# Mixture-of-experts kernel: tokens of two pairs of experts gathered at once, through a one-hot matrix of 256 columns

## What is computed

```python
def hier_moe(h, w_group, b_group, w_expert, b_expert, w1, w3, w2):
    # g_sel: best of 4 groups; e_id: best 2 of the 8 experts in that group; e_w: their weights
    y = grouped_expert_ffn(xf, e_id, w1, w3, w2)
    return einsum('nkd,nk->nd', y, e_w)

def ffn(xb, e):                       # xb: the tokens that chose expert e
    return (silu(xb @ w1[e]) * (xb @ w3[e])) @ w2[e]
```

## Time and profile before

| | us |
|---|---|
| median of 3 runs | 2134.16 (2133.64 to 2135.18) |
| span of the profiled execution | 2134.4 |
| PE busy | 2069.4 (97%) |
| DVE busy | 1592.3 (75%) |
| ACT busy | 1286.2 (60%) |
| POOL busy | 104.7 (5%) |
| mixer | up to about 1100 |
| pairs 1 to 14 | about 1181 to 2032 |
| last pair and the end | about 2032 to 2134 |

### The profile page before, as it was taken

One profiled execution on the slowest core, in us unless ns is written; L12 is line 12 of the kernel. 1 busy time (PEld: TensorE's weight loads), 2 busy tenths in 40 slices (PEclk: granted clock), 3 DMA queues, 4 the chain that ended last, 5 costly groups with the idle time before them and its releaser, 6 DMA issues.

```text
span 2134.4 us, 30028 instructions
## 1 busy us (share of the span) xinstructions
PE 2069.4 (97%) x11452; PEld 1749.8 (82%) x11452; DVE 1592.3 (75%) x1450; ACT 1286.2 (60%) x1064; POOL 104.7 (5%) x76
## 2 busy tenths in 40 slices
PE   8999999999999999999999999999999999999986
PEld 8998888899999998887887777777777787777764
DVE  7646664453646375455669999999999999999988
ACT  5445653333333323334347888888888888888883
POOL 1000000000000000001000000000000000000010
PEclk9999999999999999999999999999999999999998
DMA  6554335655454544557777999999999999999996
GB/s 215 159 139 158 118 120 186 208 180 172 146 176 148 166 157 143 192 197 239 233 297 287 399 421 421 421 420 419 418 420 418 421 418 417 417 417 418 417 397 251
DMA packets 168608, 606.48 MB, mean 284 GB/s; under 512 B 20252, under 2 KB 32684, under 8 KB 117452
## 3 DMA queue, kind: packets, MB, share of 16 engines
q1 hardware_dynamic: 164976, 598.01, 73.9%
q0 software_dynamic: 3552, 7.37, 1.1%
HBM read 595.05 MB, written 22.04 MB: 289 GB/s over the span
## 4 chain that ended last, share of the span: by engine, by line
PE 64%; DVE 16%; issue 9%; DMA 7%; ACT 3%; DVEq 0%; POOLq 0%; POOL 0%; SPq 0%; ACTq 0%
PE ps L1991 19%; PE ps L1972 15%; DVE wl L786 11%; DMA raw<-in_w_dram 7%; PE ps L1119 5%; PE ps L1120 5%; PE ps L2349 4%; PE ps L1116 3%; ACT wh L636 2%; PE ps L2104 2%; PE ps L1141 1%; DVE yall L951 1%; PE ps L2064 1%; PE ps L1089 1%; PE ps L2077 1%
## 5 line engine op out<-in xcount | busy, mean ns | idle before, releaser
L786 DVE TENSOR_TENSOR wl<-raw,wh 128x2048 fp32r<-128x2048 f32 x347 | 780.9, 2288 | 39.7 <-ACT wh L636 38.4
L636 ACT ACTIVATE wh<-raw 128x2048 fp32r<-128x2048 f32 x347 | 661.6, 1915 | 132.8 <-DMA raw<-in_w_dram 72.6
L1548 DVE TENSOR_TENSOR wl<-raw,wh 128x2048 fp32r<-128x2048 f32 (+1 forms) x168 | 379.8, 2263 | 283.3 <-ACT wh L1350 283.3
L1350 ACT ACTIVATE wh<-raw 128x2048 fp32r<-128x2048 f32 (+1 forms) x168 | 317.9, 1895 | 444.6 <-DMA raw<-in_w_in_dram 264.7
L1119 PE MATMUL ps<-wh,xg 128*128 128x512 f32 x896 | 373.1, 416 | 25.0 <-DVE wl L786 24.5
L1120 PE MATMUL ps<-wl,xg 128*128 128x512 f32 x880 | 345.2, 392 | 0.0
L1972 PE MATMUL ps<-hth,wh 128*128 128x272 f32 (+1 forms) x896 | 259.8, 290 | 3.1 <-DVE wl L1548 1.8
L1972 PE MATMUL ps<-htl,wh 128*128 128x272 f32 (+1 forms) x896 | 255.7, 285 | 0.0
L1972 PE MATMUL ps<-hth,wl 128*128 128x272 f32 (+1 forms) x896 | 255.6, 285 | 0.0
L1119 PEld LDWEIGHTS ps<-wh,xg 128*128 128x128 f32 x896 | 169.1, 189 | 77.2 <-DVE wl L786 28.3
L1119 PE MATMUL ps<-wh,hx 128*128 128x512 f32 x508 | 202.4, 398 | 3.5 <-DVE wl L786 1.9
(11 more groups left out here) (379 smaller groups left out, 3116.7 us busy)
## 6 DMA issues: line engine op xcount, KB each, us to landing
raw<-in_w_dram SPq DMA_DIRECT2D x380, 1024.0 KB, 10.4
raw<-in_w_in_dram SPq DMA_DIRECT2D x103, 1024.0 KB, 5.1
raw<-in_w_pa_dram SPq DMA_DIRECT2D x16, 1024.0 KB, 5.0
raw<-in_w_pb_dram SPq DMA_DIRECT2D x16, 1024.0 KB, 5.0
raw<-in_w_out_dram SPq DMA_DIRECT2D x16, 1024.0 KB, 5.1
raw<-in_w_ukv_dram SPq DMA_DIRECT2D x8, 1024.0 KB, 5.3
raw_e<-in_w_dram SPq DMA_DIRECT2D x4, 1024.0 KB, 8.1
yscr<-zeros SPq DMA_DIRECT2D x4, 1024.0 KB, 10.7
```

Source lines behind the costliest of these rows:

```text
L636: nc.scalar.activation(wh2[:, x % HELD, :], raw_of(turn, x), ACT.Copy).then_inc(s_wh2, 1)
L786: nc.vector.tensor_tensor(wl_of(turn, x), raw_of(turn, x), wh2[:, x % HELD, :].bitcast(F32), ALU.subtract).then_inc(s_wl2, 1)
L1350: nc.scalar.activation(wh[:, n % RING1, 0:c], raw1[:, n % RING1, 0:c], ACT.Copy).then_inc(s_wh, 1)
L1548: nc.vector.tensor_tensor(wl[:, n % RING1, 0:c], raw1[:, n % RING1, 0:c], wh[:, n % RING1, 0:c].bitcast(F32), ALU.subtract).then_inc(s_wl, 1)
```

## The change

The tokens of two pairs are gathered together, and only in pairs with an odd number n (`quad_next`): in pair 1 for pairs 2 and 3, in pair 3 for 4 and 5, up to pair 13 for 14 and 15. DVE builds one matrix of 256 columns (`gather_matrix_quad`, two operations of the old size at step 1 of an odd pair). PE does 16 portions (`gather_quad`), one for each chunk of the model width, after the steps 3 to 10 and 15 to 22 of the odd pair (`G_QUAD`); each has four matmuls of 256 columns. ACT copies each portion (`gathered_quad`) in one operation of 512 columns to two places of `xg`, which now has room for three pairs in rotation (n % 3). The pair with an even number has no gather. Pair 1 is still gathered during pair 0 in the old way.

For the rotation by three and the parity of two, the loop is written out over six pairs on PE, ACT and DVE (`cycles`, two turns), with pairs 0, 1, 14 and 15 written out before and after it. Counted in instructions of PE, weight loads included, the body of the loop grows from 1256 (two pairs) to 3389 (six pairs). Buffers move in SBUF, and `ln2g` lies where ring buffer 4 was, so that SP waits for unit 20 of the last pair before it loads it. Some waits on PE change: `mix` waits for `s_hp` and for the last portion of a gather in its banks, and the steps 0 to 3 of an even pair wait for four more chunks each.

```diff
-        xg = place("xg", [P, 2, KD, 2, 2 * SLOTS], 131072, F32R)
+        xg = place("xg", [P, 3, KD, 2, 2 * SLOTS], 131072, F32R)
-        hx = place("hx", [P, KF, 2 * SLOTS], 163840, F32R)
-        hx2 = place("hx2", [P, KF, 2 * SLOTS], 131072, F32R)
-        yall = place("yall", [P, D_MODEL], 165888)
+        hx = place("hx", [P, KF, 2 * SLOTS], 180224, F32R)
+        hx2 = place("hx2", [P, KF, 2 * SLOTS], 147456, F32R)
+        yall = place("yall", [P, D_MODEL], 196608)
...
-        selt = place("selt", [P, SEQ], 133120)
-        identr = place("identr", [P, P], 134144, F32R)
-        evens = [place("even_hi", [P, D_MODEL], 174080, F32R), place("even_lo", [P, D_MODEL], 135168, F32R)]
-        ln2g = place("ln2g", [P, D_MODEL], 196608)
+        selt = place("selt", [P, SEQ], 149504)
+        identr = place("identr", [P, P], 150528, F32R)
+        evens = [place("even_hi", [P, D_MODEL], 172032, F32R), place("even_lo", [P, D_MODEL], 151552, F32R)]
+        ln2g = place("ln2g", [P, D_MODEL], 4 * 8192)
...
-        ab = place("ab", [P, 2, FF], M0)
-        sg = place("sg", [P, 4 * SLOTS], M0 + 4096)
-        hv = place("hv", [P, KF, SLOTS], M0 + 5120)
-        zeros = place("zeros", [P, 4 * SLOTS], M0 + 5120)
-        pg = place("pg", [P, TT, 2 * SLOTS], M0 + 11712, F32R)
+        ab = place("ab", [P, 2, FF], M0 - 1024)
+        sg = place("sg", [P, 4 * SLOTS], M0 + 3072)
+        hv = place("hv", [P, KF, SLOTS], M0 + 4096)
+        zeros = place("zeros", [P, 4 * SLOTS], M0 + 4096)
+        pg = place("pg", [P, TT, 4 * SLOTS], M0 + 5120, F32R)
...
-        G_AT = (4, 6, 8, 10, 16, 18, 20, 22)
+        G_QUAD = {**{3 + c: c for c in range(8)}, **{7 + c: c for c in range(8, KD)}}
+        CYCLE = 6
+        MATRICES = 2 + (PAIRS - 2) // 2
...
+        def quad_slots(n):
+
+            return sorted((n % 3, (n + 1) % 3))
+
+        def quad_next(n, last):
+
+            return n % 2 == 1 and not last
+
+        def cycles(eng, turn, pair):
+
+            with eng.Fori(0, (PAIRS - 4) // CYCLE) as i:
+                for m in range(CYCLE):
+                    pair(turn + 2 + CYCLE * i + m, CYCLE * i + 2 + m, 2 + m)
...
                             done(sp, turn + PAIRS - 1, 16 + 2 * t + r)
                         sp.dma_start(yrow[:, t, r, :],
                                      yscr[SEQ * r + P * t:SEQ * r + P * (t + 1), :]).then_inc(s_y[2 * t + r], 16)
+                if isinstance(turn, int):
+                    done(sp, turn + PAIRS - 1, 20)
...
-            def gathered(g, par, q, bank=None):
+            def gathered_quad(g, n, c):
+
+                act.wait_ge(s_gt, 8 * g + c + 1)
+                a, b = quad_slots(n)
+                nc.scalar.activation(xg[:, a:b + 1:b - a, c, :, :],
+                                     ps[:, 7 - c % 2, :].rearrange("p (i a c) -> p i a c", i=2, a=2),
+                                     ACT.Copy).then_inc(s_xg, 1)
+
+            def gathered(g, n, q, bank=None):
 
                 act.wait_ge(s_gt, 8 * g + q + 1)
-                nc.scalar.activation(xg[:, par, 2 * q:2 * q + 2, :, :],
...
-                    for q in range(8):
-                        if k == (G_FIRST if first else G_AT)[q] and not last:
-                            gathered(turn + 1, 1 - par, q)
+                    if first and k in G_FIRST:
+                        gathered(turn + 1, n + 1, G_FIRST.index(k))
+                    if k in G_QUAD and quad_next(n, last):
+                        gathered_quad(turn + 1, n + 1, G_QUAD[k])
...
-                pair(turn, 0, first=True, early=early)
-                pair(turn + 1, 1)
-                with act.Fori(1, PAIRS // 2 - 1) as i:
-                    pair(turn + 2 * i, 0)
-                    pair(turn + 2 * i + 1, 1)
-                pair(turn + PAIRS - 2, 0)
-                pair(turn + PAIRS - 1, 1, last=True, rounds=rounds)
+                pair(turn, 0, 0, first=True, early=early)
+                pair(turn + 1, 1, 1)
+                cycles(act, turn, pair)
+                pair(turn + PAIRS - 2, PAIRS - 2, PAIRS - 2)
+                pair(turn + PAIRS - 1, PAIRS - 1, PAIRS - 1, last=True, rounds=rounds)
...
+            def gather_matrix_quad(g, col, n):
+
+                need(dve, s_gt, 8 * g)
+                slots = slots2[:, :].rearrange("p (a s) -> p a s", a=2).unsqueeze(1).broadcast_to([P, TT, 2, SLOTS])
+                at = quad_slots(n)
+                for i in range(2):
+                    ranks = rk_[:, :, bass.ds(col + 2 * i, 2)].unsqueeze(3).broadcast_to([P, TT, 2, SLOTS])
+                    c = 2 * SLOTS * at.index((n + i) % 3)
+                    m = nc.vector.tensor_tensor(pg[:, :, c:c + 2 * SLOTS].rearrange("p t (a s) -> p t a s", a=2), slots,
+                                                ranks, ALU.is_equal)
+                m.then_inc(s_pg, 1)
...
-                    if k == 1 and not first and not last:
-                        gather_matrix(turn + 1, 2 * p + 2)
+                    if k == 1 and quad_next(n, last):
+                        gather_matrix_quad(turn + 1, 2 * p + 2, n + 1)
...
-                with dve.Fori(1, PAIRS - 1) as p:
-                    pair(turn + p, p)
-                pair(turn + PAIRS - 1, PAIRS - 1, last=True)
+                pair(turn + 1, 1, 1)
+                cycles(dve, turn, pair)
+                pair(turn + PAIRS - 2, PAIRS - 2, PAIRS - 2)
+                pair(turn + PAIRS - 1, PAIRS - 1, PAIRS - 1, last=True)
...
-            def gather(g, q, *waits):
-
-                pe.wait_ge(s_pg, g + 1)
+            def gather_quad(g, c, matrix, products):
+
+                if c == 0:
+                    pe.wait_ge(s_pg, matrix)
+                need(pe, s_hp, products)
+                need(pe, s_xg, 8 * g + max(c - 1, 0))
+                bank = ps[:, 7 - c % 2, :].rearrange("p (e h s) -> p e h s", e=4, h=2)
+                for h, src in enumerate((xh1, xl1)):
+                    for t in range(TT):
+                        m = nc.tensor.matmul(bank[:, :, h, :], src[:, t, c, :],
+                                             pg[:, t, :].rearrange("p (e s) -> p e s", e=4),
+                                             start=t == 0, stop=t == 1, skip_group_check=True)
+                m.then_inc(s_gt, 1)
+
+            def gather(g, q, matrix, *waits):
+
+                pe.wait_ge(s_pg, matrix)
...
+                need(pe, s_hp, j)
...
+                quad = n % 2 == 0 and not first
                 for x in body(first):
                     k = step(x, first)
                     j = 2 * turn
                     if early and k < 4:
                         pe.wait_ge(s_xg, 2 * k + 2)
-                    elif k == 0:
+                    elif quad and k < 4:
+                        pe.wait_ge(s_xg, 8 * turn + 4 * k + 4)
+                    elif k == 0 and n < 2:
                         pe.wait_ge(s_xg, 8 * turn + 8)
...
                     if k == 0 and not first:
-                        mix(turn - 1, j - 1, 1)
+                        mix(turn - 1, j - 1, 1, *([(s_xg, 8 * turn + KD)] if quad else []))
                     if k == (14 if early else 12):
-                        mix(turn, j, 0, *([(s_hp, j), (s_stc, rounds)] if last else [(s_xg, 8 * (turn + 1) + 4)]))
+                        mix(turn, j, 0, *([(s_stc, rounds)] if last else [(s_xg, 8 * (turn + 1) + 4)] if first else
+                                          [(s_xg, 8 * (turn + 1) + 8)] if quad_next(n, last) else []))
                     if k == 20 and last:
-                        mix(turn, j + 1, 1, (s_hp, j + 1))
+                        mix(turn, j + 1, 1)
...
-                    for q in range(8):
-                        if k == (G_FIRST if first else G_AT)[q] and not last:
-                            gather(turn + 1, q, *([(s_hp, j if q < 2 else j + 1)] if q in (0, 1, 4, 5) else []))
+                    if first and k in G_FIRST:
+                        q = G_FIRST.index(k)
+                        gather(turn + 1, q, MATRICES * (rounds - 1) + 2,
+                               *([(s_hp, j if q < 2 else j + 1)] if q in (0, 1, 4, 5) else []))
+                    if k in G_QUAD and quad_next(n, last):
+                        c = G_QUAD[k]
+                        matrix = MATRICES * (rounds - 1) + p // 2 + 3
+                        gather_quad(turn + 1, c, matrix if cycle is None else matrix + CYCLE // 2 * cycle,
+                                    j if c < 8 else j + 1)
...
-                with pe.Fori(1, PAIRS // 2 - 1) as i:
-                    pair(turn + 2 * i, 0)
-                    pair(turn + 2 * i + 1, 1)
-                pair(turn + PAIRS - 2, 0)
-                pair(turn + PAIRS - 1, 1, last=True, rounds=rounds)
+                pair(turn + 1, 1, 1, rounds=rounds)
+                with pe.Fori(0, (PAIRS - 4) // CYCLE) as i:
+                    for m in range(CYCLE):
+                        pair(turn + 2 + CYCLE * i + m, 2 + m, 2 + m, rounds=rounds, cycle=i)
```

(37 more changed lines are left out.)

5 lines of the change are left out of this document (3 added, 2 removed).

## The result

The changed kernel takes **2165.23 us** (median of four runs, 2158.36 to 2168.1) against 2134.55 us before in the same comparison: a ratio of 1.014, 95% interval 1.0123 to 1.0156. That is 30.7 us more where 1 us more was forecast, and outside the range of 2129 to 2140.

The account below looks back on a forecast made before the run. The prediction took the DMA stream of weight loads to set the pace from pair 1 on. PE's savings counted as nothing, so 2134.16 us plus 0.9 for code fetches gave 2135.1 us, range 2129 to 2140.

Parts of the forecast that it names:

- What bounds the kernel: Loop from pair 1 on: the DMA stream sets the pace at 60.8 us a pair, PE next with 1 to 2 spare.
- PE, the gather: PE in odd pairs: 256-column matmuls 0.125 us apart, 9.0 us per two pairs instead of 14.4, 38 us off PE in all.
- What those 38 us are worth: nothing: Loop: PE time saved gains 0 us, since loads issued earlier only stand longer in the DMA queue.
- the queue's cover: Loop: the never-empty DMA queue hides PE's savings; without it the floor is DVE's 58.1 us, plus 0.4 in odd pairs.
- PE's clock falls: Even pairs: PE's waits lower its clock, 1.3 us a drop, slack of 8.9 us takes in six; about 2140, chance 0.02.
- The 6.5 us of the queue cover: Jump back to the loop body's head: engines may stand a few us, which the load queue's 6.5 us of slack hides.
- Code: Written-out loop: about 27 more instruction blocks of 16 KB to fetch, costing 0 to 1.9 us, taken as 0.9.
- Odd pairs: Odd pairs: 16 ACT copies and PE's gather end PE some 2 to 3 us late, without reaching the loads.
- Start and end: Pair 0 unchanged, last pair tied to the stream, `ln2g` landed by 2111 before DVE reads it at 2120.89: cost 0.
- What would show it: Profile signs: right if float32 units stay 60.8 us apart at 418 to 422 GB/s, wrong if odd pairs' DMA share falls under 1.0.
- Loads that take longer to land in even pairs (11 to 13 us): Even pairs: a sign that the forecast is right, weight loads taking 11 to 13 us to land.
- pairs shorter than 60.4 us (the loads followed PE): Loop: a sign that the forecast is wrong, pairs under 60.4 us meaning that the loads had followed PE.

Follow-up runs that it names:

- idle matmuls at two places: The changed kernel, loop written out over twelve pairs, twelve idle matmuls after steps 11 and 23 of even pairs and step 11 of the last: 2137.68 us.
- the kernel with one turn: The changed kernel with its loop written out over twelve pairs instead of six, so that no jump back is taken: 2147.22 us.
- the kernel with less gather: The kernel before, with one of eight matmuls left in each gather portion of even pairs except pair 0, the rest left out: 2145.55 us.

## Why the prediction was wrong

- **What bounds the kernel: right for the kernel before, half right for the changed one.** With the clock held up (idle matmuls at two places) it runs at 418 GB/s, with float32 units 60.3 to 61.0 us apart in most pairs. But ACT waits for loads mainly in even pairs. In odd ones PE sets the pace, at nearly the stream's: its work there was put at 60.9 us and is 60.3.
- **PE, the gather: right.** The new matmuls start 0.115 to 0.12 us apart (0.125 taken), and from the start of a portion to the matmul behind it it is 0.47 us (median of 112; 0.56 taken). In 1260 to 2050 us the kernel with one turn has PE busy for 740.5 us, 30 us less than before, though the lowered clock pads it.
- **"What those 38 us are worth: nothing": right as far as it goes.** With neither a lowered clock in the loop nor a jump, no kernel with the new gather beat the one before. The floor named for the case that the queue's cover is gone, DVE's 58.1 us, was too low: the engines need 60.05 (the kernel with less gather). But I should have asked in which form PE would get them back, and that was as stands, which are not harmless.
- **The rival "PE's clock falls": here is the step that failed.** I saw the one wait of 2.68 us and the clock of 0.74 behind it, and wrote that "a drop like that costs 0.26 x 5 = 1.3 us of PE's time; the 8.9 us of slack in an even pair take in six of them". The price of a short drop was about right: 1.3 us forecast, and 29.8 us became 31.3, which is 1.5. The cover was wrong. Slack over a pair is no store: PE spends it while it waits in front of DVE's late unit, and what it loses behind the wait falls into the two units, mix and float32 unit, where ACT and DVE wait for PE even at full clock (2.5 us in a pair). The ring of four `wh` buffers lets ACT no further ahead, and the odd pair behind, full of PE work, gives nothing back. Second, I took each drop to be as short as the one that I had seen. Behind three of the waits of the profiled run the clock was 0.50 to 0.54 for 5 us, and the float32 units stand 34.7 to 35.0 us apart there. Third, the number of drops: a stand of 2.6 us twice in every even pair was to be read from the order of work, since DVE's 2.34 us of output copy stands ahead of both. The case deserved a large part of the chance: an estimate with about 14 stands at 1.3 us, the price of the earlier trace rows, gives 2153, and at 4.5 us, which only the result shows, 2198.
- **"The 6.5 us of the queue cover" the jump: wrong.** The stand is 4.1 us, well under 6.5, and still cost 4.3 us. SP issues a load when PE is done with a unit, so during the stand one load goes out, for the unit done just before it, and then none, and DVE, which has 2.7 us to spare in a pair, is thrown back 4.26 us by way of ACT. The cover has to be held against the narrowest of the chain's links and not against the widest. The Trainium skill (Runtime: NRT & Kernel Launch, Instruction fetch mechanics) says that a branch outside the fetched window makes the engine wait for the fetch; the 4.06 us of issue at the jump agree, and I had cited that rule and priced it at nothing.
- **Code: the count right, the price too small.** There are 23 blocks more where 27 were counted, and they cost 2.8 to 3.9 us instead of 0.9. The transfer of the blocks, which the prediction priced, accounts for about 0.9; why the rest is lost stays open.
- **Odd pairs: right in time, partly by luck. Start and end: right.** Odd pairs take 60.8 us with 16 copies on ACT, but PE's work fills them instead of the wait for loads, and that the two are equally long is chance. The last pair and the end cost nothing.
- **What would show it.** "Loads that take longer to land in even pairs (11 to 13 us)" came out the other way: 8.7, 9.5 and 10.0 us (medians) in pairs 2, 4 and 6, against 10.4 before. It is the first sign that buffers came free late and not early. The sign "pairs shorter than 60.4 us (the loads followed PE)" doesn't tell the cases apart: the kernel before with idle matmuls in its last pair has two pairs of 60.05 us at 420 and 421 GB/s.

## What to carry to other kernels

Before work is taken off an engine that isn't the bottleneck, work out where it will stand instead, and for how long at once. Here PE's stands of 2.6 us cost 10.8 us in the kernel from which nothing was taken but work, and in the changed kernel twelve idle matmuls in each stand, or idle matmuls spread over the pair so that the stand never forms, took that cost away. Slack counts only behind the place where the delay arises and on the narrowest link (here DVE's 2.7 us), and lost time comes back no faster than the next limit allows (here 0.75 us in a pair, or nothing). A longer loop body has a price of its own: the body of 3389 PE instructions had a stand of 4.1 us at its jump back, and the body of 1256 none that the profile shows.

## What the runs showed of the hardware

- After stands of 2.3 to 2.7 us behind full work the granted clock fell in most cases but not in all: 13 of 15 in the changed kernel, 9 of 15 with one turn, and never after the sixteen stands of about 1.25 us with idle matmuls at two places. Two stands of 2.60 and 2.59 us in the same run, at 1431.11 and 1523.66, differ (0.78 and 1.00). What decides between them, and why the mean clock differs between runs of the same kernel (0.989 at 2147 us, 0.976 at 2172), stays open.
- The DMA share hides a loss of throughput. With one turn and no idle matmuls it is 1.01 over 1260 to 2050 us as before, while the rate is 414 instead of 419 GB/s.
- A matmul of 256 columns behind another starts 0.115 to 0.12 us later, one of 128 columns 0.105. The Trainium skill (TensorE: Matmul & The Clock Gate, Back-to-back issue gap) gives 109 and 56 ns for an isolated one: it fits the wide form and is half of what the narrow form takes here. The section says itself that this gap counts too little for few columns.
